# A hybrid decoder step on one core: K and V projected head by head inside the page steps, running softmax over groups of four pages

## The reference

```python
q, k, v = split(rmsnorm(h) @ w_qkv)            # layer 0: differential attention with ALiBi
s = (q / sqrt(128)) @ k.T - slope * dist       # -1e30 where the key lies ahead
p = softmax(s)                                 # over past pages and new tokens
a = p[:, :, 0] - lam * p[:, :, 1]              # two sub-heads per head
h += (rmsnorm(a @ v) * (1 - lam0)) @ w_o
h += swiglu(rmsnorm(h))                        # both layers; d_ff 5632
h += pool_mix(rmsnorm(h))                      # layer 1: trailing-window means, one matrix per group
y = rmsnorm(h)                                 # also returned: new K and V rows, pooling states
```

## Time and profile before

| | us |
|---|---|
| median of 3 runs | 3311.54 (3309.74 to 3311.66) |
| profiled execution | 3310.63 |
| its span | 3308.8 |
| TensorE busy | 3147.1 (95%) |
| VectorE busy | 1527.0 (46%) |
| ScalarE busy | 1054.8 (32%) |
| page loop (457.4 to 1194.0) | 736.6 |

### The profile page before, as it was taken

How to read it: one execution, slowest core, us unless ns; L and a number is a source line. 1 busy time by engine, 2 the same in 40 slices (tenths; PEclk the granted TensorE clock), 3 DMA queues, 4 the chain that set the end, 5 groups by cost and what they waited for, 6 DMA issues and landing times.

```text
span 3308.8 us, 60352 instructions
## 1 busy us (share of the span) xinstructions
PE 3147.1 (95%) x26221; PEld 2967.6 (90%) x26221; DVE 1527.0 (46%) x2015; ACT 1054.8 (32%) x1384; POOL 123.1 (4%) x127
## 2 busy tenths in 40 slices
PE   5999988898898989999999999999999999999998
PEld 4999976666666669999999999999999999999998
DVE  4333334444444335444444444445644444444445
ACT  3232223333333333322323222223523332333333
POOL 0000000000000002000000000002200000000002
PEclk8999999999999989999999999999999999999999
DMA  4344357999999964544444444443344444444442
GB/s 147 126 150 140 127 214 242 381 402 381 380 399 382 404 239 145 168 136 151 132 149 140 140 140 142 144 144 119 118 155 145 152 153 146 148 153 151 144 152 96
DMA packets 338948, 635.29 MB, mean 192 GB/s; under 512 B 10200, under 2 KB 256063, under 8 KB 304703
## 3 DMA queue, kind: packets, MB, share of 16 engines
q1 hardware_dynamic: 335778, 617.91, 52.7%
q0 software_dynamic: 1824, 11.23, 1.0%
q10 hardware_dynamic: 1084, 2.29, 0.2%
HBM read 622.62 MB, written 9.23 MB: 191 GB/s over the span
## 4 chain that ended last, share of the span: by engine, by line
PE 87%; DVE 7%; ACT 3%; issue 2%; DMA 1%; POOL 0%; ACTq 0%; SPq 0%; DVEq 0%; POOLq 0%
PE ps L1406 71%; PE ps L1491 7%; PE ps L1509 3%; PE ps L1530 2%; DVE halves L934 1%; ACT halves L669 1%; DMA raw<-in_cache_v_dram 1%; PE ps L1567 1%; DVE sc L1103 1%; PE ps L1548 1%; DVE q_n L1113 1%; ACT pa_s L781 0%; DVE pa_s L1149 0%; PE ps L1699 0%; DVE pa_n L1153 0%
## 5 line engine op out<-in xcount | busy, mean ns | idle before, releaser
L934 DVE TENSOR_TENSOR halves<-raw,halves 128x2048 fp32r<-128x2048 f32 x331 | 758.8, 2293 | 793.6 <-ACT halves L669 793.5
L669 ACT ACTIVATE halves<-raw 128x2048 fp32r<-128x2048 f32 x332 | 634.9, 1912 | 1080.0 <-PE ps L1406 1062.5
L1406 PE MATMUL ps<-xhi,halves 128*128 128x320 f32 (+1 forms) x3840 | 861.9, 311 | 7.4 <-DVE xlo L1218 5.1
L1406 PEld LDWEIGHTS ps<-xhi,halves 128*128 128x128 f32 x3840 | 650.3, 189 | 8.5 <-issue 7.3
L1406 PE MATMUL ps<-yhi,halves 128*128 128x336 f32 x2816 | 657.1, 317 | 0.1
L1406 PE MATMUL ps<-xlo,halves 128*128 128x320 f32 (+1 forms) x1920 | 598.5, 312 | 0.0
L1406 PEld LDWEIGHTS ps<-yhi,halves 128*128 128x128 f32 x2816 | 483.1, 188 | 0.5 <-issue 0.4
L1406 PE MATMUL ps<-ylo,halves 128*128 128x336 f32 x1408 | 447.1, 318 | 0.0
L1406 PE MATMUL ps<-hA_hi,halves 128*128 128x336 f32 (+1 forms) x1408 | 375.5, 314 | 2.9 <-DVE hT L1290 2.9
L1406 PE MATMUL ps<-hB_hi,halves 128*128 128x336 f32 (+1 forms) x1408 | 372.8, 312 | 0.0
L1406 PEld LDWEIGHTS ps<-xlo,halves 128*128 128x128 f32 x1920 | 362.5, 189 | 0.1
(11 more groups left out here) (183 smaller groups left out, 2671.3 us busy)
## 6 DMA issues: line engine op xcount, KB each, us to landing
raw<-in_w_gate_up_dram SPq DMA_DIRECT2D x176, 1024.0 KB, 5.0
raw<-in_w_down_dram SPq DMA_DIRECT2D x88, 1024.0 KB, 5.1
raw<-in_cache_k_dram SPq DMA_DIRECT2D x74, 1024.0 KB, 9.2
raw<-in_cache_v_dram SPq DMA_DIRECT2D x74, 1024.0 KB, 8.0
page<-in_cache_k_dram SPq DMA_DIRECT2D x54, 1024.0 KB, 9.0
page<-in_cache_v_dram SPq DMA_DIRECT2D x54, 1024.0 KB, 8.2
raw<-in_w_qkv_dram SPq DMA_DIRECT2D x48, 1024.0 KB, 5.1
raw<-in_w_o_dram SPq DMA_DIRECT2D x16, 1024.0 KB, 5.6
```

Source lines behind the costliest of these rows:

```text
L669: act.activation(whi[t][:, :], raw[r][:, :], ACT.Copy).then_inc(hi_ready[t], 1)
L934: dve.tensor_tensor(wlo[t][:, :], raw[r][:, :], whi[t][:, :].bitcast(F32), ALU.subtract)\
L1406: mm = pe.matmul(out, l, r, start=first and n == 0, stop=last and n == 2)
```

## The change

- Units: `U_K` and `U_V` are gone; Q is projected first.
- Opening: SyncE loads the input rows in two halves, ScalarE the page table and the constants in two pieces. The turned input is split as it arrives, with the norm's gain only (`xhi`, `xlo` straight from PSUM); its row factor `r0` multiplies the outputs of Q, K and V. The residual `hT` isn't kept: its place holds K/V weights, and it is loaded and turned again at steps 124 to 131 (`io2_tm`, `turn_back`).
- K and V are projected feature by feature in 16 blocks, two per head (96 matmuls of 336 columns each), through small units of 0.5 MB (3 raw buffers, whose place takes the low part, and 2 high parts). Blocks 0 and 1 come ahead of the loop, the others in chunks of six matmuls in the steps, 15 steps per head. A finished block is scaled by `kv_features`, turned by `turn_block` and copied by `kv_rows`, then stored.
- Softmax: scores of four pages form a group (three buffers of 512), with its own maximum, exponential and sum. `turn_probs` becomes a plain transpose, five steps behind the scores, in the bank of the scores; `values` lag six steps and add over four pages; VectorE rescales and adds into `o_all`. New tokens are handled apart at steps 106 to 122; `join_halves` does the sub-head difference for two sequences at a time.
- Slots for pages: 4 instead of 7. The loop has 134 steps. Prompt tiles begin one step earlier.

```diff
+SLOTS = 4
+GROUP = 4
+TURN_LAG, VALUE_LAG = 5, 6
+STEPS = PAGES + VALUE_LAG
-PA0 = 2
+PA0 = 1
+KV_STEPS = 15
+K_QUOTA = (3, 3, 2, 2, 2, 2, 2, 0)
+V_QUOTA = (3, 3, 3, 3, 2, 2, 0)
...
# ScalarE and VectorE, opening
+                act.activation(xhi[:, c, :], ps[b][:, 0:T], ACT.Copy, scale=gain_of(0, c)).then_inc(norm_hi, 1)
+                act.activation(sq0[:, c, :], ps[b][:, 0:T], ACT.Square).then_inc(squares, 1)
+                if c == 3:
+                    split_hi(U_Q)
+                if c == 11:
+                    split_hi(U_Q + 1)
...
+                dve.scalar_tensor_tensor(out=xlo[:, c, :], in0=ps[b][:, 0:T], scalar=gain_of(0, c),
+                                         in1=xhi[:, c, :].bitcast(F32), op0=ALU.mult, op1=ALU.subtract)\
...
# SyncE
+                if n >= KV_RAW:
+                    sp.wait_ge(kv_used, n - KV_RAW + 1)
+                sp.dma_start(kv_raw[n % KV_RAW][:, :].rearrange("p (c n) -> p c n", c=4),
+                             wqkv[512 * part:512 * part + 512, col:col + VD].rearrange("(c p) n -> p c n", p=P))\
...
# VectorE in the loop
+            def maxima(g):
+                dve.wait_ge(s_out, GROUP * (g + 1))
+                dve.tensor_reduce(group_max[0], sc[g % 3][:, :], AX.X, ALU.max).then_inc(smax_step, 1)
...
+            def add_values(g):
+                i = g // GROUP
+                dve.wait_ge(v_done, GROUP * (g + 1))
+                dve.scalar_tensor_tensor(out=o_all[:, i, :], in0=o_all[:, i, :], scalar=shrink(g), in1=ps[3][:, 0:VD],
+                                         op0=ALU.mult, op1=ALU.add).then_inc(o_upd, 1)
...
# TensorE
+            def turn_probs(v):
+                g = v // GROUP
+                pe.wait_ge(sexp, 2 * g + 2)
+                pe.wait_ge(s_out, min(v + TURN_LAG, PAGES - 1) + 1)
+                if v:
+                    pe.wait_ge(pt_out, v)
+                at = PAGE * (v % GROUP)
+                pe.transpose(ps[2][:, 2 * P:3 * P], sc[g % 3][:, at:at + PAGE], ident).then_inc(pt_full, 1)
...
+            def project(block, cc):
+                n, b = 4 * block + cc // 4, 6 if block == 1 else 4
+                if cc == 0:
...
+                        pe.wait_ge(kv_act, 2 * block)
+                        pe.wait_ge(kv_dve, 2 * block)
+                if cc % 4 == 0:
+                    pe.wait_ge(kv_split, n + 1)
+                at = 256 * (cc % 4)
+                for e in range(2):
+                    lo = at + P * e
+                    mm = three(ps[b + e][:, 0:T], kv_hi[n % KV_HI][:, lo:lo + P], kv_lo[n % KV_RAW][:, lo:lo + P],
+                               xhi[:, cc, :], xlo[:, cc, :], cc == 0, cc == DC - 1)
...
+            for t in range(-1, STEPS):
+                chunks = list(KV_AT.get(t, ()))
                 if tile_at(t, 3) is not None:
                     tile_turn(tile_at(t, 3))
                 if tile_at(t - PHASES, 0) is not None:
                     tile_back(tile_at(t - PHASES, 0))
                 if t + 1 < PAGES:
                     turn_keys(t + 1, 0)
+                for block, cc in chunks[0:1]:
+                    project(block, cc)
                 if 0 <= t < PAGES:
+                    scores(t)
+                for block, cc in chunks[1:2]:
+                    project(block, cc)
                 if t + 1 < PAGES:
                     turn_keys(t + 1, 1)
+                if t - VALUE_LAG >= 0:
+                    values(t - VALUE_LAG)
+                for block, cc in chunks[2:]:
+                    project(block, cc)
+                if t - 2 in NEW_AT:
+                    new_values(NEW_AT[t - 2])
+                if t in NEW_AT:
+                    new_scores(NEW_AT[t])
+                if 0 <= t - TURN_LAG < PAGES:
+                    turn_probs(t - TURN_LAG)
+                if t - 1 in NEW_AT:
+                    turn_new_probs(NEW_AT[t - 1])
+                if t in KV_END:
+                    turn_block(KV_END[t])
```

More of the change, by code:

```diff
@@ L292, in trunk @@
         stage = [place(f"stage{i}", [P, P]) for i in range(2)]
-        combs = [place(f"combs{i}", [P, H * NT]) for i in range(2)]
+        combs = stage
         gain_rows = place("gain_rows", [96, P], F32, b_at + 8192)
@@ L1472, in _, with input_ready @@
-            fm_phase(U_Q, "qg", lambda cc: None)
-            tm_phase(U_V, "vg")
+            for c in range(4):
+                turn_in(c)
+            def input_ready(cc):
+                if cc + 4 < DC:
+                    turn_in(cc + 4)
+                pe.wait_ge(*chunk_done(0, cc))
+            for e in range(2):
+                take("qg", e, 0)
+            fm_block(U_Q, 0, 0, (0, 1), input_ready, 0)
+            pe.wait_ge(ones_set, 3)
+            pe.wait_ge(lams_in, 96)
+            take("in", 4, 4)
@@ new lines, in _ @@
+            for e in range(2):
+                mm = pe.matmul(ps[4][:, P * e:P * e + P], ones[0:1, :], stage[e][0:1, :], start=True, stop=True)
+            mm.then_inc(bank_full[4], 1)
+            pe.wait_ge(lam_ready, 1)
+            take("in", 5, 4)
+            pe.matmul(ps[5][:, 0:1], ones[0:1, :], lsc[0:1, 4:5], start=True, stop=True).then_inc(bank_full[5], 1)
+            take("n0", 7, 0)
+            pe.wait_ge(sums, sums_n(0, DC - 1))
+            pe.matmul(ps[7][:, 0:T], ones[:, :], acc0[:, :], start=True, stop=True).then_inc(bank_full[7], 1)
@@ new lines, in turn_block @@
+            def turn_block(block):
+                b = 6 if block == 1 else 4
+                src = vTh if block % 2 else kTh[block // 2 % 2]
+                pe.wait_ge(kv_fm, 2 * block + 2)
+                for e in range(2):
+                    for t in range(3):
+                        r = ROWS[t]
+                        mm = pe.transpose(ps[b + e][0:r, P * t:P * t + P], src[:, e, P * t:P * t + r], ident)
+                mm.then_inc(kv_turned, 1)
+            for block in range(2):
+                for cc in range(DC):
+                    project(block, cc)
@@ L1475, in _ @@
+            for block in range(2):
+                turn_block(block)
             for b in range(4):
@@ new lines, in join_halves @@
+            def join_halves(p):
+                pe.wait_ge(comb_set, 2 * p + 2)
+                pe.wait_ge(pa_done, TILES)
+                for e in range(2):
+                    i = 2 * p + e
+                    pe.wait_ge(o_upd, GROUP * (i + 1))
+                    pe.wait_ge(n_upd, NEW_SEQ.index(i) + 1)
+                if p:
+                    pe.wait_ge(o_out, 2 * p)
+                for e in range(2):
+                    mm = pe.matmul(ps[6][:, 0:VD], combs[e][:, :], o_all[:, 2 * p + e, :], start=(e == 0), stop=(e == 1))
+                mm.then_inc(o_full, 1)
```

1036 lines of the change are left out of this document (604 added, 432 removed).

## The result

The changed kernel takes 3289.84 us (median of 4 runs, 3287.91 to 3295.19) against 3311.6; the ratio is 0.9937, 95% interval 0.992 to 0.9954. It is faster, by 22 us where 50 were forecast. Its profiled execution took 3295.19 us. Run again beside the experiments it gave 3289.76 and 3286.34 us, ratios 0.9911 (0.9879 to 0.9943) and 0.9908 (0.9882 to 0.9933).

The account below looks back on a forecast made before the run. It took TensorE, with its waits for softmax work and the lower clock after them, to bound the loop. Loop start 201.5 plus loop 942 gave 1143.5 instead of 1194.0, 50.5 us less: 3260 us, range 3190 to 3325.

Parts of the forecast that it names:

- What comes back ahead of the loop: Stretch before the page loop: opening, Q, blocks 0 and 1; loop would begin near 201.5 us instead of 457.4.
- seven blocks of 14.8 us: Q projection from its second block on: seven blocks at 14.8 us, with 3 us of slow clock, ending at 170.
- (a): Page steps without a third chunk: the probabilities' turn waits for the scores' bank, 0.22 us in 86 steps, 19 us.
- (b): Prompt-tile steps: TensorE waits for the tile's join on VectorE, 3.2 us per head, 26 us in all.
- (c): Tile softmax steps: waits of 1.85 us at a block end and 1.7 for a late key copy, 25 us in all.
- (e): New-key steps: TensorE waits for the same step's exponentials, 8 us; last 29 steps without chunks stall as before, 6 us.
- 14 blocks x 96 x 0.154 = 207 us: TensorE work added to the page loop by the K and V projection matmuls of 14 blocks, 207 us.
- The reload at nothing: Late in the loop: 3 MB of input counted only in the loop's 306 MB of transfers, with no wait added.
- Transfers and the four slots: Page loop: pages landing near 5 us cost nothing; the rival, landing in 9.2 us, said 140 us, 3400, chance 0.05.
- Transfers free ride: Rival: transfers bound the loop all along, so projections cost nothing; loop 765 us, total 3083, chance 0.03.
- Covered waits: Rival: waits (a) to (d) vanish in the seven heads with chunks, 65 us; total 3195, chance 0.15.
- Slower by the clock: Rival: 24 tiles and 14 block ends each cost a clock drop in the loop, 99 us; total 3359, chance 0.10.

Follow-up runs that it names:

- e1_q_order: Changed kernel with VectorE splitting the next even Q weight unit before it reads out the finished block, not after; 3264.39 us.
- e10_two_products: Changed kernel without one of the three products (low weights times high x) of the K and V projection from the third block on; 3247.14 us.
- e4_thin_projection: Changed kernel keeping only the high times high product of the K and V projection from the third block on; 3210.06 us.
- e3_reload_spread: Changed kernel with the five input loads for the residual issued at steps 106, 107, 111, 115 and 118, not together at 106; 3279.58 us.
- a1_changed_again: The changed kernel run once more, with no edit against it; 3289.76 us.

## Why the prediction was off by 30 us

The forecast was a saving of 50 us and the measured one is 22. What failed is the sum's term for the Q blocks, and with it two parts that the sum held at nothing: the reload, and the clock behind the loop.

- **What comes back ahead of the loop: wrong, +24.5 us.** The failed term is "seven blocks of 14.8 us", with the hand-over from block to block at nothing. The opening was right (first Q matmul 21.55, forecast 22; second block 59.46, forecast 63). The seven Q blocks from the second on took 136.5 us, 59.46 to 196.00, 18.1 to 20.4 each, where 7 x 14.8 and 3 us of slow clock gave 106.6: +29.9. The second block was 3.5 earlier than forecast and blocks 0 and 1 took 30.0 instead of 31.5; with 0.4 that I had lost in rounding to 170, together +24.5. I had read the diff for the front as moved work and did not walk VectorE's new loop in order, as I had done for the page step. Edit e1_q_order returned 27 us.
- **The loop, 942 forecast, 939.8 measured: right in length, and partly by terms that cancel.** I had 823 us of work and 119 of waits; the rows show 862.0 busy and 77.9 idle. For (a), in a step with no chunk between, the probabilities' turn began 1.15 us after the values did, where values alone take 1.00: 0.15, where (a) said 0.22. Of the terms with rows: (b) 16.6 us in the heads, forecast 26; (c) 9.8 for seven block ends, 1.4 each where 1.85 was said, and the late key copy behind a split 2.5 instead of 12; (e) 7.1, forecast 8. All were in the right place and too dear. The steps with chunks took 765.2 us, in sets of fifteen 106.8 to 110.4 (forecast 109). In work I was short by 39 us, 862 against 823. The mis-sized term is "14 blocks x 96 x 0.154 = 207 us", a pace taken from unbroken stretches: cut into chunks the same matmuls took 240 us, 33 more. The hand-over is about 0.11 us for each of 224 chunks, and shortened chunks pay it as well: in e10_two_products four matmuls take 0.73 us, in e4_thin_projection two take 0.48. Why it takes that long, no run shows. Time at half clock outside the chunks adds some 8, and smaller terms take 2 back. That too little work and too many waits gave the right length is luck.
- **The reload at nothing: wrong, some 6 to 10 us.** I had costed the 3 MB of input in the sum of bytes, not at its instant, when it stands beside chunkless steps that draw pages fastest. The two waits of 5.20 and 5.05 us and e3_reload_spread show it. These microseconds are inside the 939.8, where the waits that came out cheaper hide them.
- **The part behind unchanged: wrong, +12.8 in the profiled execution.** Its instructions are unchanged; its clock was not. This compares one profiled execution with one; in runs it comes and goes, and how much of it is in the two medians stays open.
- **Transfers and the four slots: right here, for a wrong reason.** I took pages to land in near 5 us; the median was 6.5 for keys and 8.1 for values. The cost at nothing came true in the steps with chunks. In the kernel before, with its short step, the same ring costs 57 us. This rival was much nearer than its chance of 0.05 said.
- **Transfers free ride: fell.** The loop moves 326 GB/s, and leaving work out does shorten it.
- **Covered waits: fell as a whole.** But (b) and (c) came to 29 us instead of 51, so part of them was covered.
- **Slower by the clock: fell.** The loop's clock is 0.99, better than the 0.96 of the earlier trace rows. Of its sixteen waits for pa_a the fourteen of up to 1.47 us left the clock at 1.00; behind the two longest, 3.04 and 1.66 us, it fell (0.68 and 0.66 over the next 5 us). My reading that only a wait like the 4.37 us one brings it down was wrong, though: the kernel before already had clocks of 0.50 to 0.69 over the 5 us behind its three pa_a waits of 1.94 to 2.14 us, which I hadn't looked at. It also fell elsewhere: 0.93 in the Q blocks with six waits of 3.3 us, and about 2 us instead of 1.0 for eight transposes behind the waits of 5 us. The Trainium skill, "TensorE: Matmul & The Clock Gate", section "HAM oscillation — how this bites in real kernels", describes waits that come again and again, each longer than the burst of matmuls before it, so that every burst starts at the low clock. The trace shows the low clock outside that pattern too: in the Q blocks the bursts last 15 us and the waits 3.3, and it came behind four of the six. The loop, where I had set that rule, lost some 13 us to the clock (its mean is 0.986 before rounding), not 99.

## What to carry to other kernels

Walk every engine's order in every stretch that a change rewrites, the short ones too: a weight split placed behind the read-out of the finished block cost 27 us in seven blocks, more than the whole measured gain. A pace read from an unbroken stretch is too cheap for work that is cut into short bursts: add the hand-over, here about 0.11 us for each burst. A bulk transfer with no hurry should be issued in pieces, since it delays the transfers beside it (key pages 13.6 us instead of 6.2 in the same stretch). A ring of few slots that costs nothing in one kernel can cost 57 us in another, so price it in the kernel in which it is used.

## What the hardware showed that I had not expected

- The same 128 small matmuls, with the same 2.1 us wait ahead, ran at full clock in some executions (15.3 us) and wholly or mostly at half clock in others (23 to 28 us), although TensorE was busy throughout; the runs of the changed kernel spread by 18 us beside the filled one. Filling that wait with 2 us of idle matmuls narrowed the spread to 5 and 7 us.
- Adding TensorE work to a loop raised its mean clock, 0.96 before and 0.99 after; taking two thirds of that work out brought back 0.96.
- Waits of one length did not always have one effect: of six waits of 3.30 us four were followed by the low clock, and the wait of 1.66 us for pa_a was followed by it in the changed kernel's first profile (0.66 over the next 5 us) and not in a1_changed_again (1.00).
